# Queries, attention steps and output projection woven together with the layer-1 MLP units; final norm moved to a later stage

## The reference, cut to what matters

```
layer 0:  h += even_mixer(rmsnorm(h))      # gated spatial MLP and a Mamba-2 scan, one input and one output projection
          h += squared_relu(rmsnorm(h) @ w_up0) @ w_down0        # 1024 -> 4096 -> 1024
layer 1:  qkv = rmsnorm(h) @ w_qkv + b_qkv        # 16 query heads of 64, 2 key and value heads
          scores over the last 128 keys, softmax with a learned sink per head
          h += (probs @ v) @ w_o + b_o
          h += squared_relu(rmsnorm(h) @ w_up1) @ w_down1
out = rmsnorm(h) * final_norm_g
```

## Time and profile before

| what | value |
|---|---|
| median of 3 runs | 3962.57 us (3959.99 to 4072.83) |
| the profiled execution's own time | 3957.6 us |
| its span, slowest core (core 4) | 3956.1 us |
| spans of the 8 cores | 3942.7 to 3956.1 us |
| mean granted TensorE clock of core 4 | 0.962 of full |
| PE busy | 3477.1 us (88%) |
| DVE, ACT, POOL busy | 51%, 40%, 15% |
| chain that ended last | PE 67%, DVE 13%, issue 8%, ACT 7%, DMA 4% |

### The profile page before, as it was taken

One profiled execution on the slowest core, in us unless ns is written; L12 is line 12 of the kernel. 1 busy time (PEld: TensorE's weight loads), 2 busy tenths in 40 slices (PEclk: granted clock), 3 DMA queues, 4 the chain that ended last, 5 costly groups with the idle time before them and its releaser, 6 DMA issues.

```text
span 3956.1 us, 62925 instructions; the slowest of 8 cores (3942.7 to 3956.1 us)
## 1 busy us (share of the span) xinstructions
PE 3477.1 (88%) x20246; PEld 1691.7 (43%) x20624; DVE 2015.8 (51%) x3672; ACT 1577.0 (40%) x3722; POOL 585.5 (15%) x754
## 2 busy tenths in 40 slices
PE   5777788988989989898898988899898998989888
PEld 2433344434444444444444444444444444444443
DVE  6643665445654355544655447443565436554442
ACT  3411455125551355414454155522555134541443
POOL 1411103110130110301012010211003011030100
PEclk8889699989999999999999999999999999999999
DMA  9679366886544435243343334334142432524223
GB/s 193 108 136 173 86 154 138 166 187 146 164 129 152 152 97 189 78 171 127 105 157 108 142 120 145 112 130 155 74 171 97 155 133 80 177 102 150 79 96 139
DMA packets 145594, 531.23 MB, mean 134 GB/s; under 512 B 9600, under 2 KB 83584, under 8 KB 96512
## 3 DMA queue, kind: packets, MB, share of 16 engines
q1 hardware_dynamic: 71440, 453.25, 32.6%
q0 software_dynamic: 73840, 73.93, 14.0%
HBM read 531.34 MB, written 69.73 MB: 152 GB/s over the span
## 4 chain that ended last, share of the span: by engine, by line
PE 67%; DVE 13%; issue 8%; ACT 7%; DMA 4%; POOL 1%; DVEq 0%; ACTq 0%; POOLq 0%; SPq 0%
PE ps L785 20%; PE ps L781 16%; PE ps L1002 6%; DVE scr L1418 4%; PE ps L1030 3%; PE ps L837 3%; PE ps L1113 3%; PE ps L900 3%; PE ps L877 2%; DMA rm<-w_down 2%; ACT scr L1299 2%; DVE ast L1599 2%; PE ps L809 2%; ACT yTm L1232 2%; PE ps L757 1%
## 5 line engine op out<-in xcount | busy, mean ns | idle before, releaser
L1150 ACT ACTIVATE hid<-ps 128x512 bf16<-128x512 f32 x512 | 305.8, 597 | 762.9 <-DVE ps L1377 738.9
L1382 DVE TENSOR_TENSOR h<-ps,h 128x512 f32<-128x512 f32 x512 | 351.0, 687 | 392.5 <-PE ps L785 392.5
L785 PE MATMUL ps<-rd,hid 128*128 128x512 bf16 x1951 | 480.2, 386 | 53.1 <-ACT hid L1150 33.2
L781 PE MATMUL ps<-yTd,rd 128*128 128x512 bf16 x1959 | 477.3, 386 | 52.0 <-ACT hid L1150 21.8
L785 PE MATMUL ps<-rm,hid 128*128 128x512 bf16 x2008 | 458.2, 382 | 26.0 <-DMA rm<-w_down 19.5
L781 PE MATMUL ps<-yTm,rm 128*128 128x512 bf16 x2008 | 453.1, 383 | 25.5 <-DVE rm L1350 15.8
L1299 ACT ACTIVATE scr<-ps,ast 128x256 bf16<-128x256 f32 x512 | 237.9, 470 | 354.2 <-DVE ast L1601 340.6
L1377 DVE TENSOR_SCALAR ps<-ps 128x512 f32<-128x512 f32 x256 | 179.0, 699 | 275.2 <-PE ps L781 275.2
L785 PEld LDWEIGHTS ps<-rm,hid 128*128 128x128 bf16 x2048 | 200.7, 98 | 274.9 <-issue 48.6
L781 PEld LDWEIGHTS ps<-yTm,rm 128*128 128x128 bf16 x2048 | 201.1, 99 | 271.6 <-issue 38.1
L785 PEld LDWEIGHTS ps<-rd,hid 128*128 128x128 bf16 x2048 | 196.6, 99 | 270.8 <-issue 81.3
(11 more groups left out here) (202 smaller groups left out, 4713.7 us busy)
## 6 DMA issues: line engine op xcount, KB each, us to landing
rm<-wscr_m SPq DMA_DIRECT2D x226, 1024.0 KB, 5.1
rd<-wscr_d SPq DMA_DIRECT2D x104, 1024.0 KB, 5.0
wscr_m<-rm SPq DMA_DIRECT2D x34, 1024.0 KB, 9.7
rm<-w_down POOLq DMA_DIRECT2D x16, 1024.0 KB, 23.5
wscr_d<-rd SPq DMA_DIRECT2D x16, 1024.0 KB, 10.0
rd<-w_down POOLq DMA_DIRECT2D x16, 1024.0 KB, 10.4
out<-h SPq DMA_DIRECT2D x32, 512.0 KB, 10.7
scr<-x SPq DMA_DIRECT2D x28, 512.0 KB, 6.7
```

The costliest lines, as they stand in the source:

```text
L781: m = pe.matmul(bk, lhsT=w[:, k, (r % 4) * 128:(r % 4 + 1) * 128], rhs=yT[:, k, :], start=k == 0, stop=k == 7)
L785: m = pe.matmul(bk, lhsT=hid[:, k, what[1] * 128:(what[1] + 1) * 128], rhs=w[:, k, :], start=k == 0, stop=k == 7)
L1150: act.activation(out=hid[:, what[1], :], in_=bk, func=AF.Square).then_inc(*a_hid[L].inc(t, 8 * q + what[1]))
L1382: dve.tensor_tensor(out=hv, in0=bk, in1=hv, op=ALU.add).then_inc(*v_mu[L].inc(t, 8 * q + r - 8 if L else u))
```

## The change

The plan, the five engine functions and the waits between them are rewritten around the attention; the amount of arithmetic is the same.

- The keys and values come first, then queries 0-2 as a block, and queries 3-7 after attention steps 0-4, one each. Queries use banks 6 and 7.
- Steps 0-4 have no side unit. Steps 5-33 have one each (step 32 two), except steps 13, 14, 21, 22, 29 and 30, which have the output projection of the chunk behind instead (`project`, banks 6 and 7). Only the projection of chunk 3 stays in the tail. Side units in attention: 24 as before.
- The tail is `tl0` (two side units), `tl1` (projection of chunk 3, norms d0 and d1), `tl2` (two side units, norm d2). In the conv stage the first side unit is at `cv5`; it was at `cv4`, and `cv5` had none.
- `held(t)`: on ACT, at the start of an attention step and of a conv step the held-back unit is issued before that step's own work. DVE does so at `at33` and in the tail.
- Final norm of tile t-2 instead of t-1: sums of squares on ACT at `u1`-`u4`, inverse roots on POOL at `u2`-`u5`, scaling on DVE at `u5`-`v0`. SP stores tile t-2 and loads tile t at `u7`. Those of tile NT-2 come before the last 64 units on ACT and DVE, and its store at the end of SP's queue.
- The last quarter of the side units takes chunks 0 and 1 with both halves, then 2 and 3, in an order that changes the weight block every two units.

Core of the diff:

```
-        add("at%d" % n, 1 if n < 32 and n % 4 else 0)
+        add("at%d" % n, 0 if n < 5 or (n >= 13 and n % 8 in (5, 6)) else 2 if n == 32 else 1, [M_WO, M_WO + 1] if n == 13 else [])
+        if n < 5:
+            q(n + 3)
     for i in range(5):
-        add("tl%d" % i, 1 if i < 4 else 0, ...)
+        add("tl%d" % i, (2, 0, 2, 0, 0)[i], [], [M_WO, M_WO + 1] if i == 1 else [])
...
# SP
-                if name == "tl4":
-                    if t:
-                        store_out(t - 1)
-                    if t + 1 < NT:
-                        load_h(t + 1)
+                if name == "u7" and t:
+                    if t >= 2:
+                        store_out(t - 2)
+                    load_h(t)
...
# PE, side units
+                if t + 1 < NT and u - u % 2 == NEXT_Q:
+                    pe.wait_ge(*a_q.at(t + 1, 7 + u % 2))
+                elif t + 1 < NT and u - u % 2 in NEXT_WO:
+                    pe.wait_ge(*v_wp.at(t + 1, 2 * NEXT_WO.index(u - u % 2) + u % 2))
...
# PE, new
+            def query(i):
+                w = view_m(t, M_Q + i // 4)
+                if i % 4 == 0:
+                    pe.wait_ge(*ready_m(t, M_Q + i // 4))
+                if i >= 2:
+                    pe.wait_ge(*a_q.at(t, i - 1))
+                else:
+                    pe.wait_ge(*(hidden_free(t - 1, NEXT_Q - 2 + i, 1) if t else gm_r.at(7)))
+                for k in range(8):
+                    m = pe.matmul(bank(6 + i % 2), ...)
+            def project(tc, n):
+                ...
+                if n == 0:
+                    pe.wait_ge(*a_ao.at(t, tc))
+                if t:
+                    pe.wait_ge(*hidden_free(t - 1, NEXT_WO[tc] - 2 + n, 1))
+                for k in range(8):
+                    m = pe.matmul(bank(6 + n), lhsT=aoT[:, tc, k, :], rhs=w[:, k, :], start=k == 0, stop=k == 7)
...
+                if n >= 13 and n % 8 in (5, 6):
+                    project(n // 8 - 1, n % 8 - 5)
...
# ACT
+        def held(t):
+            for u in late:
+                unit(t - 1, u, 1)
+            late[:] = []
...
+                if t >= 2 and 1 <= i <= 4:
+                    if i == 1:
+                        act.wait_ge(*added(t - 2, 63, 1))
+                    final_sq(t - 2, i - 1)
...
# DVE
-                if name == "tl4":
-                    final(t - 1, 3)
+            if t >= 2 and name in ("u5", "u6", "u7", "v0"):
+                final(t - 2, ("u5", "u6", "u7", "v0").index(name))
```

More of the change, by code:

```diff
@@ L112 @@
 SIDE = {p[0]: p[3] for p in PTS}
+NEXT_Q = SIDE["at5"][0]
+NEXT_WO = [SIDE[n][0] for n in ("at15", "at23", "at31", "tl2")]
+assert all(u % 2 == 0 for u in NEXT_WO + [NEXT_Q])
 FIRST = {p[0]: p[1] for p in PTS}
@@ L741, in pool_program @@
                 pt(t, name)
+        if NT >= 2:
+            for c in range(4):
+                final(NT - 2, c)
         for u in range(64):
@@ L1050, in heads_t @@
                 m.then_inc(*p_ao.inc(t, tc))
-            pe.wait_ge(*a_q.at(t, 8))
-            pe.wait_ge(*v_v.at(t))
+            for i in range(3):
+                query(i)
             for n in range(34):
@@ L1314, in scalar_program @@
                     act.activation(out=aoT[:, 3, :, :], in_=bank16(3).rearrange("p (j t) -> p j t", t=128), func=AF.Copy).then_inc(*a_ao.inc(t, 3))
-                if i:
-                    norm_sq("d", t, i - 1)
+                if i == 2:
+                    norm_sq("d", t, 2)
                 pt(t, "tl%d" % i)
-        for u in late + list(range(64)):
+                if i == 2:
+                    norm_sq("d", t, 3)
+        held(NT - 1)
+        if NT >= 2:
+            act.wait_ge(*added(NT - 2, 63, 1))
+            for c in range(4):
+                final_sq(NT - 2, c)
+        for u in range(64):
             unit(NT - 1, u, 1)
@@ L1382, in unit, with held @@
                 dve.tensor_tensor(out=hv, in0=bk, in1=hv, op=ALU.add).then_inc(*v_mu[L].inc(t, 8 * q + r - 8 if L else u))
-                if L and q == 3 and what[2] == 1 and what[1]:
+                if L and t == NT - 1 and q == 3 and what[2] == 1 and what[1]:
                     final(t, what[1] - 1)
         late = []
+        def held(t):
+            for u in late:
+                unit(t - 1, u, 1)
+            late[:] = []
         def pt(t, name):
@@ L1395, in pt @@
             if t:
-                for u in late + SIDE[name][:-1]:
+                held(t)
+                for u in SIDE[name][:-1]:
                     unit(t - 1, u, 1)
                 late[:] = SIDE[name][-1:]
-                if name == "tl4":
-                    final(t - 1, 3)
+            if t >= 2 and name in ("u5", "u6", "u7", "v0"):
+                final(t - 2, ("u5", "u6", "u7", "v0").index(name))
         for c in range(4):
@@ L1585, in vector_program @@
             norm_e("c", t, 3)
-            for i in range(8):
-                pt(t, "q%d" % i)
-            dve.wait_ge(*p_q.at(t, 9))
+            dve.wait_ge(*p_q.at(t, 0))
             if t:
@@ L1592, in vector_program, with project @@
             pt(t, "kv")
+            for i in range(3):
+                pt(t, "q%d" % i)
+            def project(tc, n):
+                dve.wait_ge(*p_wp.at(t, 2 * tc + n))
+                if n == 0:
+                    dve.wait_ge(*g_bo.at(t, tc))
+                hv = h[t % 2][:, tc, n * 512:(n + 1) * 512]
+                dve.tensor_tensor(out=hv, in0=bank(6 + n), in1=hv, op=ALU.add).then_inc(*v_wp.inc(t, 2 * tc + n))
             for n in range(34):
```

241 lines of the change are left out of this document (134 added, 107 removed).

## The result

The changed kernel takes 3789.31 us, median of four runs (3783.34 to 4221.83), against 3964.52 for the kernel before in the same session (3959.99 to 4072.83). The ratio is 0.9557 with a 95% interval of [0.9535, 0.9578]: faster, by 4.4%. The profiled execution took 3789.8 us; before it was 3957.6. In some runs of this study (the 4221.83 is one) the cores of one die were granted a lower clock than the others (in that run 0.84 in the mean against 0.97); ratios and comparisons leave those out.

The account below looks back on a forecast made before the run. PE was taken as the bound, with only its holes and slow stretches to win. 7 tiles x (20 + 4) + 12 - 2 = 178 us off 3957.6 gave 3780, own range 3745 to 3815 (chance 0.64).

Parts of the forecast that it names:

- Attention and tail: Keys and queries to the tail's end: of 25.1 us to win, 4.6 stay; gain 20 us a tile (8 to 25).
- ACT's crowding: Attention: ACT is full at some four steps a tile, 4 x 0.3 = 1.2 us late (0 to 4).
- One filler a step is enough: Attention steps: a 1.73 us filler and next score, 2.4 us, cover the 2.1 us chain by 0.3.
- Banks 6 and 7 and the held units: Attention: changes of bank user cost nothing, 1 us each (five changes) if the cover went.
- it doesn't weave: Rival, attention: bank hand-overs and held units stall PE like the old holes; only the conv gains: 3930; chance 0.06.
- Conv: Conv stage: both waits, 1.7 and 1.4 us, lose their cause; gain 4 us of 5.3 idle (0 to 5).
- Final norm in u and v: Stages u and v: the moved squares and scalings cost nothing, 5 us a tile if each square delayed a group.
- SP's queue: Stores and load moved to u7 delay weight refills; they overlap in part, so nothing, 5 us a tile otherwise.
- The rival's mechanism: Rival, side units' weights: SP's late refill costs 5 us a tile, giving 3815; chance 0.13.
- Tile 0: First tile: eleven fillers go into 14.9 idle us of attention and the tail is shorter; gain 12 us (3 to 18).
- The end: Kernel's end: four squares and scalings before the last 64 units and 2 MB more to store, -2 us (0 to -6).
- The clock rival: Attention stretch: a PE with fewer holes is granted less clock; at 0.75 the kernel takes 4053; chance 0.04, other losses included.

Follow-up runs that it names:

- sixth experiment: Changed kernel with a chunk's sum and reciprocal issued on DVE a step earlier, the last scaling ahead of the held add: 3775.22 and 3769.28 us.
- fifth experiment: Changed kernel with an extra ACT copy of the scores' bank, waited for, before each pair of exponentials: 3854.72 us.
- seventh experiment: Kernel of the sixth experiment with two side units moved from the conv to the grouped stages gm and s: 3750.9 us, in a second run 3748.93.
- eighth experiment: Kernel of the seventh experiment with two more side units moved from the conv, to gm0 and gm4: 3781.53 us.
- unaltered kernel: The changed kernel run again without any edit, beside the sixth experiment: 3788.05 us.
- third experiment: Changed kernel with all eight query groups as one block before the attention, projections still woven: 3844.76 us.
- fourth experiments: Changed kernel with all eight projection groups, and the norms d0 and d1, in the tail after step 33: 3869.13 us.
- first experiment: Kernel before with only the final norm, the store and the load moved to the u stage: 3945.98 us, ratio 0.9979.
- second: Changed kernel without the early issue of the held unit on ACT in conv and attention steps: 3841.96 us, ratio 0.9704.

## Why the prediction was right, and where it was not

3780 was forecast and 3789.3 measured, inside its own range. It comes this near partly by luck: a steady tile gained 24.9 us against 24 forecast, with 1.1 us that I had not forecast making up for the conv, and a last tile that gained more than I said covers part of what tile 0 did not give. Step by step:

- **Attention and tail, steady tile: right, term by term.** Forecast 144.0 to 124; it is 124.4. The split was 118.9 us of work at full clock, which the window gives as 118.79, and 4.6 us of waits, of which the view shows 5.5. Within them: chunk scalings 1.2 forecast, 2.6 measured; last chunk's transposes 0.8, 1.1 measured; query 1 0.4, 0.4 measured; ACT's crowding 1.2, none seen; a slow clock piece 1, none (clock 1.00); the last norm's transposes behind their scaling and one add, 1.0 and 0.4, I had not listed. The sixth experiment shows the cause of the first two, sum, reciprocal and scaling in a row on DVE: with the first two of these earlier, 3.2 of the 3.7 us go and the tile is 2.8 us shorter.
- **One filler a step is enough: right, and with about the margin I said.** I had 0.3 us between chain and PE; the fifth experiment adds 0.6 us, and a step grows by 0.24, so some 0.35. It doesn't tell whether the chain or ACT's fullness is the nearer limit. Both halves of the weaving were needed: without the queries +55 us, without the projections +80.
- **Banks 6 and 7 and the held units: right, but on one condition that I passed over.** I treated the early issue on ACT as a detail of the conv. It is worth 53 us in all, 4 us a tile in the attention alone; without it the rival "it doesn't weave" has a fair part of its way.
- **Conv: 4 forecast, 3.3 measured.** One of the two waits went, by the moved norm. I had said that both causes were removed; the unit still waits 2.0 us for the square, now with relu and square ahead of the conv output. ACT and DVE do 30 and 39 us of work in these 49 us, and a unit there costs 2.2 us instead of its 1.73 (the seventh experiment).
- **Final norm in u and v: 0, right.** z to v is 50.2 in both, PE busy 47.70 of 47.70.
- **SP's queue: 0, right, but with little to spare.** Side unit 16 starts 1.77 us late for DVE's add into h, as in the earlier trace rows, not for its block. The rival's mechanism is real: it came in as soon as the eighth experiment asked for a block earlier.
- **Tile 0: +12 forecast, nothing measured. This step failed,** outside its bounds of 3 to 18. The whole tile is 1.4 us longer in the median of the cores and 4.8 on the slowest, the clock of 0.81 included; from keys and queries to the tail's end, where no core had that clock, it is 115.6 us before, 115.9 after and 115.4 in the unaltered kernel's second profile. The step was "eleven fillers go into its 14.9 idle us". Queries and keys are 7.0 us shorter, the tail 4.4, and the attention 11.7 longer. In tile 0 a step that has neither side unit nor filler typically lasted 1.95 us before (most 1.7 to 2.3, those with a chunk's end aside), and one with a filler lasts 2.71; so a filler of 1.73 us finds not a hole of its own size but one of 1.0, and costs 0.76. Eleven of them cost 8.4. The rest of the 11.7 is not in the waits for the chunk scaling, which are 5.9 us in three now and were 5.7 in three. Three waits for a norm's pass (L1408) take 2.8 us where one took 0.6, and two of the six projections ran wholly or in part at the lower clock, instead of 1.89 us:

```profile
463.98 2.52 PE L1080 MATMUL ps<-rm,scr 128*128 128x512 bf16 x8
485.44 3.62 PE L1080 MATMUL ps<-rm,scr 128*128 128x512 bf16 x8
```

The idle us are still there:

```profile
429.50:517.30 87.80, 70.48 (x498) 34.58 (x496) 56.53 (x133) 45.95 (x153) 4.09 (x11) 0.80 0.21 57
```

87.8 less 70.5 is 17.3 us idle, more than the 14.9 of the earlier trace rows, because the unfilled steps keep theirs. The shorter tail is a bare chain, as the timeline of PE shows:

```profile
519.48 1.01 PE L1087 MATMUL ps<-ident_bf,scr 128*128 128x128 bf16 x8 [2.30 <-DVE scr L1703]
521.86 5.98 PE L1080 MATMUL ps<-rm,scr 128*128 128x512 bf16 x16 [1.37 <-ACT scr L1369]
527.67 1.06 PE L775 MATMUL ps<-ident_bf,ys 128*128 128x128 bf16 x16
531.78 0.61 PE L775 MATMUL ps<-ident_bf,ys 128*128 128x128 bf16 x8 [3.05 <-DVE ys L1402]
```

Scaling, transposes, copy, projection and norm follow each other with nothing beside them, the projection mostly at the lower clock: 5.98 us for sixteen matmuls that take 3.62 in tile 4. The third and fourth experiments agree. In tile 0 the five queries cost 4.8 us inside the attention (82.7 to 87.5) and 8.4 in their block; the six projections 8.0 inside (79.5 to 87.5) and 10.4 in the tail. The casts that I had held against the tail's gain took little of it: the conv of tile 1 waits 2.7 us for a cast block (`rd<-w_down`) where it waited 0.8.
- **The end of the MLP stage: nothing forecast, 1.1 us a tile measured,** in every woven kernel and not in the first experiment. Before, the first query needed the last norm's pass and PE waited for it; now the keys and values come first, and the products for the values of the first chunks need only the norms before. They start 0.49 us after the last transposes do, the query started 1.66 us after them:

```profile
2283.51 13.97 PE L1030 MATMUL ps<-yTm,rm 128*128 128x512 bf16 x62 [1.05 <-DVE yTm L1346]
...
2211.27 1.95 PE L1048 MATMUL ps<-rm,yTm 128*128 128x128 bf16 x32
```

- **The end: -2 forecast, a gain instead.** The last tile with the end is 27.6 us shorter, 3 more than a steady one. Before, the first of the last 64 units waited 4.7 us for the last norm's pass into `yTd` (L781 behind L1346), and on DVE that pass stood behind the last final scaling, which had to wait itself (timeline of DVE, core 4):

```profile
3828.27 1.28 DVE L1363 SCALAR_TENSOR_TENSOR h<-h,fst,bc_sb 128x1024 f32<-128x1024 f32 x1 [1.30 <-POOL fst L670]
3829.47 0.68 DVE L1346 COPY yTd<-ps 128x1024 bf16<-128x1024 bf16 x1
```

After, the wait is 0.9 us (L801 behind L1408): the final norm has left that place. The first experiment, which moves that norm alone, shows it: its last tile with the end is 5.8 us shorter than before (median of the cores), a steady tile 3.1. The four squares and scalings that I charged cost nothing that can be seen.

The clock rival fell where it had to be strongest: the attention, denser than before, rose from 0.95 to 1.00. The Trainium skill (TensorE: Matmul & The Clock Gate, Part 1, Seeing it yourself) states that once three cores of a die run dense matmuls a limiter takes the whole die to 13/16 of the clock. The profiled executions agree with it in part only. Its level is there, the 0.81 of tile 0 above, but on two of each die's four cores. And in the MLP of tile 4 all eight cores are dense, PE busy 111.2 to 113.2 of 113.70 us, and all are granted 1.00.

What stays open: I haven't separated, in the eighth experiment, how much of the 5.8 us is the late block and how much the units' own cost in gm0 and gm4. Nor have I found why some cores were granted 0.81 and others not: six of the experiments' profiles have such pieces too, and the second profile of the unaltered kernel has none.

## What to carry to other kernels

A filler is worth its length only where the hole is as long, or where the clock would otherwise fall: in steps that already ran 1.95 us apart it cost 0.76 of its 1.73 us, and in steps behind which the clock dropped, 0.16. Before weaving, add up the work of the second engine in one full step, from start to start, and see in which order it issues the filler's part and the step's own; that order alone was worth 53 us here.

## What the runs showed of the hardware that I had not expected

- The lower clock goes on into work that has no holes. After steps with one wait of 1.79 us and three of 0.33 to 0.40, eight matmuls of 128x512 took 3.62 us instead of 1.89 (third experiment), and 3.57 after one wait of 3.93 us (second). With no wait above 1.1 us the whole 124 us stretch ran at 1.00.
- The granted clock can be 0.81 on some cores of a die and 1.00 on the others at the same time in the same program (tile 0 of the changed kernel, cores 6 and 7 against 4 and 5).
- Each ACT operation with an accumulated sum is followed by a record of a read of 0.197 us (64 of them in the attention). It begins before the operation's own record ends, and the next operation starts 0.46 us after the first, the length of the operation's own record. A sum that takes 0.47 us for each exponential holds the reads already; to add their 12.6 us a tile would count them twice.
